# Shift/scale blocks alternately in full precision and split, and a new order at attention's start, in a one-core diffusion layer

## The reference

```
mod = silu(c) @ w_ada + b_ada            # for latent and context: 6 x 1024 shifts, scales, gates
h = rmsnorm(x, norm1) * (1 + scale1) + shift1
q_a, kv_a, k_r, u = split(h @ w_in)      # 256, 128, 32, 512 columns
q = rmsnorm(q_a) @ w_qb ; k, v = rmsnorm(kv_a) @ w_kvb    # 8 heads, rotary parts of 32
attn = softmax(q k^T / sqrt(96)) v       # latent: 1024 + 128 cached keys; context: its own 128
pooled = (windowed mean of u - u) @ w_pool * pool_scale   # windows 2, 4, 8, 16
x = x + gate1 * (concat(attn, pooled) @ w_o)
x = x + gate2 * (relu(h2 @ w1)^2 @ w2) ; y = rmsnorm(x, final_norm)
```

## Time and profile before

| | |
|---|---|
| median of 3 runs | 1463.22 us |
| the profiled execution | 1462.78 us |
| its span | 1460.6 us |
| TensorE busy | 1377.5 us, 94% |
| VectorE, ScalarE, GpSimd busy | 56%, 49%, 30% |
| mean granted TensorE clock | 0.984 |
| last shift/scale product ends | 47.35 us |
| first projection (L1276) starts | 54.10 us |
| first scores (L1380) start | 183.65 us |

### The profile page before, as it was taken

The page is one execution under the profiler, slowest core; times in us unless marked ns, Lnnn a source line. Parts: engine busy times, 40 slices in busy tenths (PEclk is TensorE's granted clock), DMA queues, the critical chain, the costliest instruction groups (busy, mean ns, idle before and its releaser), DMA issues.

```text
span 1460.6 us, 20549 instructions
## 1 busy us (share of the span) xinstructions
PE 1377.5 (94%) x7548; PEld 1236.6 (85%) x7548; DVE 818.7 (56%) x1206; ACT 708.7 (49%) x1416; POOL 441.9 (30%) x542
## 2 busy tenths in 40 slices
PE   5899889999999979999999999999999999999996
PEld 1599878999888858899999888899998879999995
DVE  6577577777777744245555455544445545444444
ACT  5677567787777732243333443433334433333332
POOL 3476637888778624450000001100000020000002
PEclk9899999999999989999999999999999999999999
DMA  8522001111111060053443333433333334333321
GB/s 295 168 77 78 28 17 40 42 42 42 42 37 37 25 243 1 34 219 137 160 170 129 116 115 116 159 142 115 128 130 116 116 116 159 142 115 129 130 86 43
DMA packets 50445, 154.63 MB, mean 106 GB/s; under 512 B 9832, under 2 KB 12392, under 8 KB 50376
## 3 DMA queue, kind: packets, MB, share of 16 engines
q1 hardware_dynamic: 49512, 150.60, 29.3%
q0 software_dynamic: 864, 3.15, 0.5%
HBM read 148.73 MB, written 4.83 MB: 105 GB/s over the span
## 4 chain that ended last, share of the span: by engine, by line
PE 60%; DVE 2%; POOL 1%; ACT 1%; DMA 0%; issue 0%; DVEq 0%; ACTq 0%; POOLq 0%
PE bank L2048 27%; PE bank L2040 26%; PE bank L1756 6%; POOL x L1829 1%; PE bank L1530 1%; DVE wol L1718 0%; DMA add<-in_w_o 0%; DVE w1l L1935 0%; DVE w2l L1935 0%; PE bank L1561 0%; DVE add L1979 0%; PE bank L2062 0%; ACT w2h L1866 0%; DVE rTl L1946 0%; ACT rTh L1884 0%
## 5 line engine op out<-in xcount | busy, mean ns | idle before, releaser
L2040 PE MATMUL bank<-h2h,w1l 128*128 128x384 f32 x768 | 258.2, 336 | 0.0
L2040 PE MATMUL bank<-h2l,w1h 128*128 128x384 f32 x768 | 258.2, 336 | 0.0
L2040 PE MATMUL bank<-h2h,w1h 128*128 128x384 f32 x768 | 258.2, 336 | 0.0
L1829 POOL TENSOR_TENSOR x<-x,add 128x512 f32<-128x512 f32 x16 | 20.9, 1334 | 717.8 <-DVE add L1979 717.8
L2048 PE MATMUL bank<-w2h,rTh 128*128 128x512 f32 x576 | 182.7, 398 | 7.8 <-DVE rTl L1946 7.8
L2048 PE MATMUL bank<-w2l,rTh 128*128 128x512 f32 x576 | 179.7, 393 | 0.0
L2048 PE MATMUL bank<-w2h,rTl 128*128 128x512 f32 x576 | 179.0, 392 | 0.0
L1884 ACT ACTIVATE rTh<-sq 128x384 fp32r<-128x384 f32 x94 | 49.4, 525 | 243.6 <-PE bank L2048 239.7
L1873 ACT ACTIVATE relu<-bank 128x384 f32<-128x384 f32 x94 | 46.1, 491 | 247.1 <-PE bank L2040 247.1
L1946 DVE TENSOR_TENSOR rTl<-sq,rTh 128x384 fp32r<-128x384 f32 x96 | 53.6, 558 | 174.1 <-ACT rTh L1884 169.9
L1935 DVE TENSOR_TENSOR w1l<-w1raw,w1h 128x1024 fp32r<-128x1024 f32 x94 | 117.2, 1247 | 55.2 <-ACT w1h L1866 55.2
(11 more groups left out here) (269 smaller groups left out, 2904.2 us busy)
## 6 DMA issues: line engine op xcount, KB each, us to landing
w1raw<-in_w SPq DMA_DIRECT2D x96, 512.0 KB, 3.7
w2raw<-in_w SPq DMA_DIRECT2D x96, 512.0 KB, 4.6
ada_raw<-in_w_ada SPq DMA_DIRECT2D x24, 512.0 KB, 4.8
xn<-in_w_ada SPq DMA_DIRECT2D x16, 512.0 KB, 3.5
xin<-in_x SPq DMA_DIRECT2D x9, 512.0 KB, 3.6
x<-in_x SPq DMA_DIRECT2D x3, 1536.0 KB, 12.4
g_raw<-in_w_ada SPq DMA_DIRECT2D x8, 512.0 KB, 3.5
out_y<-x POOLq DMA_DIRECT2D x6, 512.0 KB, 5.4
```

Of the source, the lines that this page charges most:

```text
L1829: nc.gpsimd.tensor_tensor(k.x[:, t, cut], k.x[:, t, cut], add[:, i, :], ALU.add).then_inc(out_added, 1)
L2040: op = nc.tensor.matmul(bank[6 + s][:, 0:BN], w[0][s][x][:, c * P:(c + 1) * P], k.h2[b % 2][y_][:, c, :], start=n == 0, stop=n == 3 * DC - 1)
```

## The change

`Modulation` has 6 raw slots. Even blocks are split as before, into two part slots of their own. Odd blocks aren't split: `multiply` takes the raw block and the unsplit silu columns in two full-precision products. An even slot may be loaded again when its low part is made, an odd one when its product is. The shift/scale loads now come first in the SP queue; x tiles 0 and 1 follow blocks 1 and 3, weight blocks 0 to 3 follow blocks 5, 7, 9 and 11, weight blocks 4 to 7 and x tile 2 come after block 15. Weight blocks 8 to 11 are split in the steps instead of ahead of them. The square of tile 2 follows the first modulation and writes elsewhere. `turn_x(0)` stands behind block 5.

At attention's start the rotary rows go in pieces: 1152 columns in step 24, the last 128 (context) at the old place; for the second head VectorE does halves in units 2 and 3. In unit 0 the first maximum and exponential stand ahead of the last poolings and the first values; in units 0 and 1 the order on TensorE of the two last `mix`, the side product and the values is new. Semaphore counts follow; one tile (`silu`) is allocated earlier.

```diff
@@ -130,51 +130,51 @@
...
+        self.hi_done, self.ready, self.done = sem("ada_hi"), sem("ada_ready"), sem("ada_done")
     def load(self, sp, n):
-        if n >= self.nr:
-            for c in range(2):
-                sp.wait_ge(self.ready[c], n - self.nr + 1)
...
-        sp.dma_start(self.raw[:, s, :], self.a["w_ada"][self.first + n]).then_inc(self.loaded[s], 16)
+        if n >= self.slots:
+            if n % 2:
+                sp.wait_ge(self.done, n - self.slots + 1)
+            else:
+                sp.wait_ge(self.ready, n - self.slots + 2)
+        s = n % self.slots
+        sp.dma_start(self.raw[:, s, :], self.a["w_ada"][n]).then_inc(self.loaded[s], 16)
     def high(self, act, n):
-        act.wait_ge(self.loaded[n % self.nr], 16 * (n // self.nr + 1))
-        if n >= self.np:
-            act.wait_ge(self.done, n - self.np + 1)
-        self.nc.scalar.activation(self.parts[0][:, n % self.np, :], self.raw[:, n % self.nr, :],
-                                  ACT.Copy).then_inc(self.hi_done, 1)
-    def low(self, eng, n, c):
-        cut = slice(c * 512, (c + 1) * 512)
-        eng.wait_ge(self.hi_done, n + 1)
-        eng.tensor_tensor(self.parts[1][:, n % self.np, cut], self.raw[:, n % self.nr, cut],
-                          self.parts[0][:, n % self.np, cut].bitcast(F32), ALU.subtract).then_inc(self.ready[c], 1)
+        act.wait_ge(self.loaded[n % self.slots], 16 * (n // self.slots + 1))
+        if n >= 4:
+            act.wait_ge(self.done, n - 3)
...
+    def low(self, eng, n):
+        eng.wait_ge(self.hi_done, n // 2 + 1)
+        for c in range(2):
+            cut = slice(c * 512, (c + 1) * 512)
+            eng.tensor_tensor(self.parts[1][:, n // 2 % 2, cut], self.raw[:, n % self.slots, cut],
+                              self.parts[0][:, n // 2 % 2, cut].bitcast(F32), ALU.subtract).then_inc(self.ready, 1)
     def multiply(self, pe, n, out):
+        first, last = n % 4 == 0, n % 4 == 3
         for c in range(2):
-            pe.wait_ge(self.ready[c], n + 1)
-            for x in range(2):
-                op = self.nc.tensor.matmul(out[0:4, :], self.k.silu[:, 2 * (n % 4) + c, :],
-                                           self.parts[x][:, n % self.np, c * 512:(c + 1) * 512],
-                                           start=n % 4 == 0 and c == 0 and x == 0, stop=n % 4 == 3 and c == 1 and x == 1,
-                                           skip_group_check=True)
+            cut, chunk = slice(c * 512, (c + 1) * 512), 2 * (n % 4) + c
+            if n % 2:
+                if c == 0:
+                    pe.wait_ge(self.loaded[n % self.slots], 16 * (n // self.slots + 1))
+                silu = self.k.sf[:, :].rearrange("p (j c) -> p c j", j=2)
+                op = self.nc.tensor.matmul(out[0:2, :], silu[:, chunk, :], self.raw[:, n % self.slots, cut],
+                                           start=False, stop=last and c == 1, skip_group_check=True)
+            else:
+                pe.wait_ge(self.ready, n + c + 1)
+                for x in range(2):
+                    op = self.nc.tensor.matmul(out[0:4, :], self.k.silu[:, chunk, :], self.parts[x][:, n // 2 % 2, cut],
+                                               start=first and c == 0 and x == 0, stop=False, skip_group_check=True)
         op.then_inc(self.done, 1)
@@ -202,7 +202,7 @@
...
-            mod = Modulation(nc, a, k, memory(nc, early), sem, 0, 4, 2)
+            mod = Modulation(nc, a, k, memory(nc, early), sem, 6)
@@ -245,8 +245,8 @@
...
-        FIRST_AT = {5: 4, 7: 5, 9: 6, 11: 7}
-        RAW_AT = {0: (12, 13), 1: (14, 15), 2: (16,)}
+        ROWS_BEHIND, WEIGHTS_BEHIND = {1: 0, 3: 1}, {5: 0, 7: 1, 9: 2, 11: 3}
+        RAW_AT = {0: (8, 9, 10), 1: (11, 12, 13), 2: (14, 15, 16)}
@@ -436,16 +436,15 @@
...
-                rows(0)
-                rows(1)
-                for n in range(4):
-                    weights(n)
                 for b in range(2 * DC):
                     mod.load(sp, b)
-                    if b == 3:
-                        rows(2)
-                    if b in FIRST_AT:
-                        weights(FIRST_AT[b])
+                    if b in ROWS_BEHIND:
+                        rows(ROWS_BEHIND[b])
+                    if b in WEIGHTS_BEHIND:
+                        weights(WEIGHTS_BEHIND[b])
+                for n in range(4, DC):
+                    weights(n)
+                rows(2)
                 for n in range(DC, DC + 4):
@@ -474,8 +473,10 @@
...
+                sp.wait_ge(sm_hi, len(turned) - 1)
+                sp.dma_start(k.krT[QK:P, 0:LKEY], k.krT[NOPE:QK, 0:LKEY]).then_inc(kr_doubled, 16)
                 sp.wait_ge(sm_hi, len(turned))
-                sp.dma_start(k.krT[QK:P, :], k.krT[NOPE:QK, :]).then_inc(kr_doubled, 16)
+                sp.dma_start(k.krT[QK:P, LKEY:NKEY], k.krT[NOPE:QK, LKEY:NKEY]).then_inc(small_loaded, 16)
                 sp.wait_ge(pf_ready, T)
                 sp.dma_start(a["new_krope"], pf[:, QL + KVL:QL + KVL + ROPE]).then_inc(stored, 16)
@@ -650,10 +651,7 @@
...
-                    if n == 5:
-                        rs_x(pool, 2)
-                for n in range(DC, DC + 4):
-                    split_lo(n)
+                rs_x(pool, 2)
                 for s in range(STEPS):
                     if s - 1 in A_AT:
@@ -699,12 +697,13 @@
...
+                    scratch = hf[:, :] if t != 2 else hT[1][1][:, :, :].rearrange("p a b -> p (a b)")[:, 0:D]
...
                                          accum_out=k.stat[:, t, 0:1]).then_inc(x_sq, 1)
@@ -853,9 +852,9 @@
...
-                def rope_rows(j):
-                    act.wait_ge(kr_doubled, 16)
-                    nc.scalar.activation(kT[j][0][NOPE:P, :], k.krT[NOPE:P, :], ACT.Copy).then_inc(setup_hi, 1)
+                def rope_rows(j, lo, hi):
+                    act.wait_ge(*((kr_doubled, 16) if hi == LKEY else (small_loaded, 64)))
+                    nc.scalar.activation(kT[j][0][NOPE:P, lo:hi], k.krT[NOPE:P, lo:hi], ACT.Copy).then_inc(setup_hi, 1)
@@ -874,20 +873,18 @@
...
-                square(0)
-                square(1)
-                for n in range(4):
-                    split_hi(n)
                 for b in range(2 * DC):
-                    mod.high(act, b)
-                    if b in FIRST_AT:
-                        split_hi(FIRST_AT[b])
-                    if b == 8:
-                        square(2)
-                for n in range(DC, DC + 4):
+                    if b % 2 == 0:
+                        mod.high(act, b)
+                    if b in ROWS_BEHIND:
+                        square(ROWS_BEHIND[b])
+                    if b in WEIGHTS_BEHIND:
+                        split_hi(WEIGHTS_BEHIND[b])
+                for n in range(4, DC):
                     split_hi(n)
                 act.wait_ge(gain_done, 4)
-                modulate(0, 3)
+                modulate(0, 2)
+                square(2)
                 for s in range(STEPS):
                     if s in M_AT:
@@ -916,11 +913,13 @@
...
+                        act.wait_ge(proj_ready, T)
+                        rope_rows(0, 0, LKEY)
                 pooled_high(13)
                 read_u(15)
                 first_query(0)
                 first_key(0)
-                rope_rows(0)
+                rope_rows(0, LKEY, NKEY)
                 first_key(1)
                 first_key(2)
@@ -928,7 +927,6 @@
...
-                pooled_high(14)
@@ -966,23 +964,27 @@
...
-                        mixed(14)
+                        pooled_high(14)
+                        exponent(0)
                         pooled_high(15)
+                    if u == 1:
+                        mixed(15)
+                        exponent(1)
                     early = list(VALUES_AT.get(u, ()))
                     for v in early[:2]:
                         high_value(v)
                     for i in turns(u)[:3] if u > 2 else ():
                         high(i)
-                    if u < NU:
+                    if 1 < u < NU:
                         exponent(u)
                     for v in early[2:]:
                         high_value(v)
+                    if u == 0:
+                        mixed(14)
                     for i in turns(u)[3 if u > 2 else 0:]:
                         high(i)
-                    if u == 0:
-                        mixed(15)
                     if u == 2:
-                        rope_rows(1)
+                        rope_rows(1, 0, NKEY)
                     if u - 1 in ADA_AT:
                         ada_latent(ADA_AT[u - 1])
@@ -1117,9 +1119,9 @@
...
-                def rope_rows(j):
-                    dve.wait_ge(setup_hi, j + 2)
-                    nc.vector.tensor_tensor(kT[j][1][NOPE:P, :], k.krT[NOPE:P, :], kT[j][0][NOPE:P, :].bitcast(F32),
+                def rope_rows(j, lo, hi, highs):
+                    dve.wait_ge(setup_hi, highs)
```

(54 more changed lines are left out.)

45 lines of the change are left out of this document (14 added, 31 removed).

## The result

The changed kernel took **1451.68 us** (median of 4 runs, 1450.18 to 1452.88) against 1461.61 of the kernel before, measured beside it (4 runs, 1459.21 to 1464.26): ratio 0.9921, 95% interval 0.9900 to 0.9942. That is faster, clear of the noise, by 0.8%. The forecast was 1449.0. The profiled execution took 1452.31 us for a span of 1450.4, 10.2 us shorter than the span before. Repeated later (e11) the same kernel gave 1449.37 (5 runs).

A forecast was written before the change was run, and what follows sets the result against it. TensorE, busy 94% of the span, bounds the kernel, so time comes only where its queue runs dry or slowly. 1462.8 - 12.9 (opening) + 1.7 (backlog) - 2.8 (attention's start) + 0.4 (median) was given as 1449.0 us, range 1443.5 to 1458.5.

The forecast's parts named there:

- Opening: Shift/scale stage: odd blocks in full precision and block loads first end the last product 12.9 us earlier.
- rival B: Loads at 279 GB/s bound the shift/scale stage: only 4.3 us gained, ending at 1457.8; chance 0.12.
- The backlog: Steps 0 to 2: weight splits moved there delay the fourth tile; 1.7 us given back, bounds 0 and 4.
- tile 4's norm behind three splits: Step 2 on GpSimd: two more splits ahead make it 2.6 us later, against 0.8 of slack at project(3).
- Attention's start: Rotary rows in pieces and new order, from first scores to the second head: 2.8 us earlier, bounds 0 and 6.
- Pieces: First head's rotary rows, nine tenths of them in step 24: first scores 1.55 us earlier.
- Pushes it by 0.6, which mix(13) just covers: Step 24 on VectorE: rotary rows in front of pooled_low(13) delay it by 0.6 us, which mix(13) just covers.
- Value(5) waits: First head's values: new wait for high_value(2), queued behind exponent(1) on ScalarE, idles TensorE about 1.6 us.
- The halved rows of the second head: Second head's rotary rows spread over two steps: maximum(3) comes 0.75 us sooner, and exponent(3) behind it.
- Rival A: Clock stays low through the shift/scale products: they end 6.9 us later, the kernel at 1469.0; chance 0.05.
- Rival C: Opening as forecast, but 4 us given back in the backlog and nothing gained at attention's start: 1454.3; chance 0.14.
- D: Shorter full-precision products, or clock high sooner and still so at attention: 3 us better, 1446 or less; chance 0.12.

The follow-up runs named there:

- e11: The changed kernel again, as it is: 1449.37 us, ratio 0.9911.
- e4: Changed kernel with weight blocks 8 to 11 split right behind tile 2's square, ahead of the second modulation, instead of in steps 0 and 1: 1451.02 us.
- e5: Changed kernel with VectorE scaling the first projection's row ahead of tile 2's split in step 1: 1453.14 us.
- e7: Changed kernel with both order edits, first row ahead of tile 2's split and fourth tile's scale factors ahead of step 2's weight splits: 1449.20 us.
- e10: The kernel of e7 again, timed beside the changed kernel on the same chip: 1448.09 us against 1449.37.
- e12: Changed kernel with the first head's rotary rows in one piece as before, keeping only the new order at attention's start: 1453.35 us.
- e1: Kernel before with the change's opening edits up to step 24 only, attention's start as before: 1457.05 us.
- e2: Kernel before with the change's attention's start edits only, opening as before: 1459.15 us.
- e8: Changed kernel with the order at attention's start undone, keeping only the rotary rows in pieces: 1454.56 us.
- e6: Changed kernel with GpSimd computing the fourth tile's scale factors ahead of the weight splits in step 2: 1450.91 us.

## Why the prediction was right, and which of its steps was not

**A slip.** The prediction's sum, 1462.8 - 12.9 + 1.7 - 2.8 + 0.4, is 1449.2; it says 1449.0.

**Opening, forecast 12.9, measured 12.4: right in its steps but for one price.** The first block was copied at 5.54 (forecast 6.0) and the products began at 7.47 (7.85). The level rose at 12.06 (13.0). A full-precision product is two records 0.43 us apart as in the earlier trace rows although its stationary operand has 2 columns: a block 1.88 at the higher clock as the profile prints it (forecast 1.72 to the next one's start, about 1.8 here). The last product ended at 35.5 (34.4). The walk from 12.45 took 23.0 us where 21.4 were forecast, because a pair of blocks took 2.83 us and not 2.64. From the last split record to the first full one it is 0.32 us (30.50 to 30.82) instead of 0.23, and back it is 0.52 instead of 0.43, so each change of form costs 0.09: seven pairs, 1.3 us. The other 0.3 are waits for VectorE's low parts, the last at 19.6 us. (The walk began 0.55 us sooner than forecast, so that 1.1 of the 1.6 show at its end.)
It was not rival B. ScalarE's copies did wait some 0.7 us each for their loads (16.82, 19.98 and on, 3.16 us apart while weight blocks came between, 1.28 MB at 405 GB/s). But the parts were ready before TensorE needed them: the last block landed at 30.13, near the forecast's 29.4, and was used at 33.66. The rate was 365 to 426 GB/s and not 279.
The Trainium skill (DMA: Bandwidth & Descriptors, "Where 436 GB/s comes from") says that transfers between HBM and SBUF are bound near 358 GB/s for a core. The trace doesn't agree: it has 18 slices in a row above that, and the measurement decides.
The low-clock time after the stage was not in the sum: 6.8 us from 39.4, in the first projection; the kernel before had its own at 50.7 to 57.5.

**The backlog, forecast 1.7 back with bounds 0 and 4, measured 4.8: the step that failed.** "ScalarE copies them where it waited for loads before, so up to block 13 nothing is late." ScalarE's copies were indeed not late. The step priced the moved splits only where GpSimd's own work stands behind them. What it left out is what they do to VectorE beside them: waiting for the weights had kept GpSimd's splits away from most of VectorE's row. At the small transposes that cost 2.15 us. The term that I did name, tile 4's norm behind three splits, is there with 1.7 (lead 9.8 to 8.1 at 83.60), and another 0.6 by 88.58, where the rest of a wait of 0.30 and slower splits lie. The last 0.5 is the clock in the first projection, 57 to 61 us. e4 shows that fewer splits in step 1 don't help, e5 that moving the row out of their reach removes that wait and creates the next one, e7 and e10 that both orders together leave 3.4 to 3.8 more of the lead at 88.58, some 3 of it at the waits.
The Trainium skill (SBUF — State Buffer, "SBUF: two separate sides") says that GpSimd and some VectorE instructions take a shared port pair as an exclusive lock for a whole instruction. The rows agree: VectorE's three instructions of 0.35, 0.28 and 0.19 us each took 1.26 to 1.36, the time of one split (1.26 to 1.72, three in 4.21). Had I asked this in the prediction, I would have looked at what each moved split lies beside, and found 3 x 1.3 - 0.8 = 3.1 us, less the 0.95 that the last instruction lost before too: about 2.15.

**Attention's start, forecast 2.8, measured 2.8 to 213.46, and 4.35 to 217.78.** That the first two agree is in part luck, since errors in both directions cancel. Pieces: the first scores 1.56 earlier (forecast 1.55). "Pushes it by 0.6, which mix(13) just covers" was wrong: mix(13) waits 0.56 and the lead falls by 0.77 there (7.60 to 6.83), which e12, without the pieces, doesn't show. The first scores ran at the higher clock, as I had assumed, and gained 1.07 by the last of them (forecast 1.3). But my reason, that the idle time ahead of them was short, isn't shown: in e1 and e12 the 2.25 us of idle time are still there and the first scores gain the same 1.03 and 1.04. So the lead won was 1.9 behind the first scores, not 2.9. Value(5) waits as foreseen, but 0.95 instead of 1.6, and at the turns the lead won was 2.2 (forecast 1.9). The halved rows of the second head gave 0.68 (forecast 0.75). Then came what the forecast had only in its upper bound: before, the clock was lower at 214.6 to 218.0; with any half of this part it is not (changed, e2, e8, e12 and all others), without it, it is (before, e1, where it comes at 209.5). Worth 1.5 us. That these belong together rests on two traces against eleven, and why it goes was not found out.

**From 218 us to the end** the lead falls by 1.7: 0.1 to 392, and the rest in stretches at the lower clock at 398 and 497 us, against one at 1191 in the kernel before. The forecast had nothing for these; e11 shows that such a stretch can come and go with the same kernel.

**The sum.** 12.9 - 1.7 + 2.8 = 14.0 forecast; 12.4 - 4.8 + 4.3 - 1.7 = 10.2 measured. One term was short by 3.1 us, and clock stretches nearly cancel (+1.5, -1.7), which is luck. Rival A fell at 12.06. Rival C was nearer in the handover (4) but named another place for it, and had attention's start wrong. D's earlier clock came true by 1 us and its 1446 is where no median was.

## What to carry to other kernels

Work moved off the critical path onto GpSimd isn't free where VectorE has short instructions on the path: list what will run beside each moved instruction, above all where it used to wait for a load, because the wait was a separation. When a wait goes and the time doesn't, look for the next instance of the same handover, one tile on, before calling the idea wrong (at 88.58 e5 alone had won nothing, e6 alone at most 0.9, both together 3.4 or more). That an engine waits for its loads doesn't make them the bound: compare when a block lands with when it is used. And where two forms of a product alternate on a busy TensorE, price the change from one to the other too.

## What was unexpected in the hardware

Short VectorE instructions took about the length of a GpSimd one: 0.19 us became 1.26. Changing between split and full-precision products with narrow stationary operands cost TensorE 0.09 us each time. The query split on GpSimd went from 2.19 to 1.00 us when VectorE's rows no longer ran beside it. The granted clock falls for single stretches at places that differ between kernels which agree in everything up to there and, at 398 us, between two executions of one; the one at 215 us cost 1.5 us, over half of what the prediction gave to attention's start.
